# Mixture-of-experts loop reordered: up product of item k+1 between up and down of item k, in two banks; second half of the gather behind the first up product

## What is computed

```python
def layer_norm(x, g, b):
    mu = jnp.mean(xf, -1, keepdims=True)
    var = jnp.mean(jnp.square(xf - mu), -1, keepdims=True)
    ...
def hier_moe(h, w_coarse, w_fine, w1, w3, w2):
    ...
    gates = jnp.einsum('tk,tke->te', w_top, jax.nn.one_hot(expert, MOE_EXPERTS, dtype=jnp.float32)).astype(x.dtype)
    hid = jax.nn.silu(jnp.einsum('td,edf->tef', x, w1)) * jnp.einsum('td,edf->tef', x, w3)
    y = jnp.einsum('tef,efd->td', hid * gates[:, :, None], w2)
    return y.reshape(b, l, d)
# per layer: x <- LN(alpha*x + gate1 * MIX(mod1(x))); x <- LN(alpha*x + gate2 * HMOE(mod2(x)))
# 32 experts, 2 chosen for each token, D_MODEL 1024, hidden width 256
```

## Time and profile before

| | us |
|---|---|
| median of 3 runs | 1191.67 |
| lowest and highest | 1188.70, 1193.04 |
| profiled execution | 1184.91 |
| its span in the trace | 1182.9 |

### The profile page before, as it was taken

How to read it: one execution, slowest core, us unless ns; L and a number is a source line. 1 busy time by engine, 2 the same in 40 slices (tenths; PEclk the granted TensorE clock), 3 DMA queues, 4 the chain that set the end, 5 groups by cost and what they waited for, 6 DMA issues and landing times.

```text
span 1182.9 us, 18088 instructions
## 1 busy us (share of the span) xinstructions
PE 1092.0 (92%) x6858; PEld 766.2 (65%) x6869; DVE 617.9 (52%) x1216; ACT 456.2 (39%) x818; POOL 67.2 (6%) x113
## 2 busy tenths in 40 slices
PE   4999999999989899999979999999998989999993
PEld 0777778787775556665558776878776555555551
DVE  0654757788654532222278385678866353222224
ACT  0634454454343223333354345635524322333332
POOL 0401000200100000000020001010000000000000
PEclk8899999999999999999989999999999999999997
DMA  9997774554899999999977876555376899999991
GB/s 352 308 334 268 269 285 148 179 197 177 322 407 408 411 408 409 409 409 409 378 212 247 306 282 249 178 181 191 139 272 265 315 410 394 410 409 409 408 376 37
DMA packets 107980, 360.08 MB, mean 304 GB/s; under 512 B 9220, under 2 KB 12768, under 8 KB 99696
## 3 DMA queue, kind: packets, MB, share of 16 engines
q1 hardware_dynamic: 97392, 301.48, 67.1%
q0 software_dynamic: 10496, 57.39, 14.0%
HBM read 356.13 MB, written 3.74 MB: 304 GB/s over the span
## 4 chain that ended last, share of the span: by engine, by line
PE 64%; DVE 14%; ACT 7%; issue 5%; DMA 5%; DVEq 3%; ACTq 1%; SPq 0%; POOL 0%; PEld 0%; POOLq 0%
PE bank L923 60%; PE bank L926 4%; DVE wl L1885 3%; ACT wh L1560 3%; DMA first<-in_w_ada 2%; ACT hidT L1832 2%; DMA raw<-in_w_in 1%; DMA adaw<-in_w_ada 1%; DVE merged L1885 1%; DVEq L2232 1%; DVE tmp L1885 1%; DVE seg L2356 1%; DVE tmp L2216 1%; DMA decay<-decay_rows 1%; DVE xbc L2151 0%
## 5 line engine op out<-in xcount | busy, mean ns | idle before, releaser
L1885 DVE TENSOR_TENSOR wl<-raw,wh 128x2048 fp32r<-128x2048 f32 (+1 forms) x76 | 169.1, 2236 | 61.5 <-ACT wh L1560 60.3
L1560 ACT ACTIVATE wh<-raw 128x2048 fp32r<-128x2048 f32 (+1 forms) x76 | 142.6, 1877 | 68.6 <-PE bank L923 48.4
L923 PE MATMUL bank<-wh,hTh 128*128 128x512 f32 x448 | 127.1, 406 | 0.5 <-ACT merged L1582 0.5
L923 PE MATMUL bank<-raw,xg 128*64 128x256 f32 x1088 | 125.1, 381 | 0.0
L923 PE MATMUL bank<-wh,hTl 128*128 128x512 f32 x448 | 121.4, 393 | 0.0
L923 PE MATMUL bank<-wl,hTh 128*128 128x512 f32 x448 | 120.0, 390 | 0.0
L923 PEld LDWEIGHTS bank<-raw,xg 128*64 128x64 f32 x1088 | 93.3, 138 | 39.8 <-issue 17.5
L923 PE MATMUL bank<-wide,xg 128*64 128x256 f32 x1024 | 116.9, 379 | 0.0
L2522 DVE TENSOR_SCALAR selT<-bank 128x256 fp32r<-128x256 f32 x66 | 28.0, 425 | 164.5 <-ACTq L1807 164.5
L923 PEld LDWEIGHTS bank<-wide,xg 128*64 128x64 f32 x1024 | 88.3, 137 | 35.9 <-issue 15.7
L923 PEld LDWEIGHTS bank<-wh,hTl 128*128 128x128 f32 x448 | 85.4, 191 | 18.8
(11 more groups left out here) (328 smaller groups left out, 1473.9 us busy)
## 6 DMA issues: line engine op xcount, KB each, us to landing
raw<-in_moe_w SPq DMA_DIRECT2D x136, 512.0 KB, 11.4
wide<-in_moe_w SPq DMA_DIRECT2D x128, 512.0 KB, 11.6
raw<-in_w_in SPq DMA_DIRECT2D x52, 1024.0 KB, 6.7
wide<-in_moe_w SPq DMA_DIRECT2D x34, 1024.0 KB, 12.9
adaw<-in_w_ada POOLq DMA_DIRECT2D x32, 1024.0 KB, 7.0
raw<-in_moe_w SPq DMA_DIRECT2D x32, 1024.0 KB, 12.6
raw<-in_w_branch SPq DMA_DIRECT2D x12, 1024.0 KB, 5.4
raw<-in_w_ada SPq DMA_DIRECT2D x8, 1024.0 KB, 9.9
```

The source lines that it names most:

```text
L923: return behind(nc.tensor.matmul(*args, **kw))
L1560: A_(wh[c][:, 0:n], raw[:, r, 0:n], ACT.Copy).then_inc(part_high[c], 1)
L1885: return V.tensor_tensor(o, a, b, op)
```

## The change

- **PE** runs up(k+1) between up(k) and turn_hidden(k), into one of two banks by turns; all of its 33 items stand ahead of the branch. At the start only the first half of the gather stands ahead of up(0). The second follows it, and item 0 is finished before up(1).
- **ACT** has all four copies of the second half, take_seats(1) and weigh(0) ahead of sil(0), and in the loop hidT(k-1), sil(k), take_seats(k+2), ygh(k-1), weigh(k+1). `next_piece(0)` stands between the items 31 and 32, as before, but hidT(31) and ygh(31) are now part of item 32's turn.
- **DVE** has low_part(k-1) (ygl) in item k, and the counts of tiles in seven lumps over items 5 to 11.
- **SP** counts a handed back piece by three counters: the first half of up, up, and down. The order of the pieces becomes 0, 1, 3, 4, 2, 6, 7, 5, 9, 10, 8, 12, 13, 11, 15, 16, 14 and so on, with 98 last. The slots are placed anew, so slot 11 is first filled by piece 11, behind 12 and 13.
- **POOL** waits in layer 1 for hT_ready ahead of its parameter loads. **Output** finishes stream 0, then the two halves of stream 1, and DVE's normalisation of stream 1 goes half by half.

```diff
-HIGH_SLOT, LOW_SLOT, RAW_SLOT = (4, 6, 2), (5, 7, 3), 8
+HIGH_SLOT, LOW_SLOT, RAW_SLOT = (6, 8, 2), (7, 9, 10), (3, 4, 5, 11)
...
-DOWN_BANK, UP_BANK, SELECT_BANK = 5, 6, 7
-GATHER_BANKS = (UP_BANK, 0, 1, DOWN_BANK)
+DOWN_BANK, SELECT_BANK = 5, 7
+UP_BANKS = (6, ADA_BANK)
+GATHER_BANKS = (UP_BANKS[1], 0, 1, DOWN_BANK)
...
-        slot = [raw4[:, :], raw5[:, :]] + [wide[i][:, :] for i in (4, 5, 0, 1, 2, 3)] + [raw[:, i, :] for i in range(SLOTS)]
+        slot = ([raw4[:, :], raw5[:, :], wide[4][:, :]] + [raw[:, i, :] for i in range(SLOTS - 1)]
+                + [wide[i][:, :] for i in (0, 1, 2, 3, 5)] + [raw[:, SLOTS - 1, :]])
...
-                return pieces_used, 3 * self.items + j + 1
+
+                k, h = j // 3, j % 3
+                return (pieces_used, up_done, down_done)[h], self.items + k + 1
+
+            def piece(self, at):
+
+                if at < 2 or at == 3 * self.n - 1:
+                    return at
+                return at + 1 if at % 3 != 1 else at - 2
...
-                for j in range(first, end):
+                for at in range(first, end):
+                    j = run.piece(at)
...
-                        sp.wait_ge(*mains[l].finished(RAW_SLOT + i))
+                        sp.wait_ge(*mains[l].finished(RAW_SLOT[i]))
...
+                    pool.wait_ge(hT_ready, 5 * l + 5)
...
+                output((0,), 0, (0, 1), False)
+                output((0,), 1, (0, 1), True)
+                output((1, 2, 3), 0, (0, 1), False)
+                output((1, 2, 3), 1, (0,), False)
+                output((1, 2, 3), 1, (1,), True)
...
+                def gather_second():
...
-                    t = bank[UP_BANK]
+                    t = bank[UP_BANKS[k % 2]]
...
-                    hand_back()
...
-                def items(run, first, end):
-
-                    for k in range(first, end):
-                        up(run, k)
-                        if run.first == 0 and k == 0 and l < L - 1:
-                            pe.wait_ge(room_filled, 2 * QUARTERS * (l + 1))
-                            turn_mod(l, 0, "adaT_next")
+                def items(run):
+
+                    up(run, 0)
+                    if run.first == 0:
+                        gather_second()
+                    if run.first == 0 and l < L - 1:
+                        pe.wait_ge(room_filled, 2 * QUARTERS * (l + 1))
+                        turn_mod(l, 0, "adaT_next")
+                    turn_selected(run, 1)
+                    for k in range(run.n):
+                        if k and k + 1 < run.n:
+                            up(run, k + 1)
+                        turn_hidden(run, k)
                         if k:
                             scatter(run, k - 1)
-                        else:
-                            turn_selected(run, 1)
-                        turn_hidden(run, k)
-                        if k and k + 1 < run.n:
-                            turn_selected(run, k + 1)
                         down(run, k)
+                        if k == 0:
+                            up(run, 1)
+                        if k + 2 < run.n:
+                            turn_selected(run, k + 2)
 
                 def one_more():
-                    items(lasts[l], BRANCH_AT, MAIN)
                     scatter(main, MAIN - 1, True)
-                    pe.sem_inc(pieces_used, 3 * MORE)
+                    pe.sem_inc(pieces_used, MORE)
...
-                        gathered(1, 0)
                         act.drain()
                         act.wait_ge(slots_known, l + 1)
                         act.sem_inc(waited, 1)
@@ -1818,23 +1841,40 @@
                         act.wait_ge(need_ready, l + 1)
                     take_seats(run, 0)
                     if run.first == 0:
-                        for p in range(1, QUARTERS):
+                        for p in range(QUARTERS):
                             gathered(1, p)
                     act.drain()
+                    take_seats(run, 1)
                     weigh(run, 0)
 
+                def hidden_turned(run, k):
+
+                    act.wait_ge(hid_turned, run.items + k + 1)
+                    A_(hidT[:, :], bank[UP_BANKS[k % 2]][:, 256:256 + P], ACT.Copy).then_inc(hidT_ready, run.step(k, MAIN - 1))
+
+                def high_rows(run, k):
+
+                    act.wait_ge(down_done, run.items + k + 1)
+                    A_(ygh[:, :], bank[DOWN_BANK][:, :], ACT.Copy).then_inc(y_high, run.step(k, MAIN - 1))
+
                 def items(run, first, end):
 
                     for k in range(first, end):
+                        if k:
+                            hidden_turned(run, k - 1)
                         act.wait_ge(up_done, run.items + k + 1)
-                        A_(sil[:, :], bank[UP_BANK][:, 0:P], ACT.Silu).then_inc(sil_done, run.step(k, MAIN - 1))
-                        act.wait_ge(hid_turned, run.items + k + 1)
-                        A_(hidT[:, :], bank[UP_BANK][:, 256:256 + P], ACT.Copy).then_inc(hidT_ready, run.step(k, MAIN - 1))
+                        A_(sil[:, :], bank[UP_BANKS[k % 2]][:, 0:P], ACT.Silu).then_inc(sil_done, run.step(k, MAIN - 1))
+                        if k + 2 < run.n:
+                            take_seats(run, k + 2)
+                        if k:
+                            high_rows(run, k - 1)
                         if k + 1 < run.n:
-                            take_seats(run, k + 1)
                             weigh(run, k + 1)
-                        act.wait_ge(down_done, run.items + k + 1)
-                        A_(ygh[:, :], bank[DOWN_BANK][:, :], ACT.Copy).then_inc(y_high, run.step(k, MAIN - 1))
+
+                def last_rows(run):
+
+                    hidden_turned(run, run.n - 1)
+                    high_rows(run, run.n - 1)
...
                     items(lasts[l], BRANCH_AT, MAIN - 1)
                     next_piece(0)
                     items(lasts[l], MAIN - 1, MAIN)
+                    last_rows(lasts[l])
                     next_piece(1)
...
+                    else:
+                        for h in range(2):
+                            hs = slice(h * 512, (h + 1) * 512)
+                            t = bank_full(dve, l, f"{out}1{h}")
+                            frees(tt(tmp[:, hs], t[:, :], gains[:, 1, hs], ALU.mult), f"{out}1{h}")
+                            drain()
+                            V.scalar_tensor_tensor(out=x[:, 1, hs], in0=x[:, 1, hs], scalar=ALPHA, in1=tmp[:, hs], op0=ALU.mult, op1=ALU.add)
+                            drain()
+                            sampled(1, h)
...
                     for k in range(first, end):
                         dve.wait_ge(sil_done, run.items + k + 1)
-                        V.scalar_tensor_tensor(out=hid[:, :], in0=bank[UP_BANK][:, P:2 * P], scalar=gg[:, k % 2:k % 2 + 1], in1=sil[:, :],
+                        V.scalar_tensor_tensor(out=hid[:, :], in0=bank[UP_BANKS[k % 2]][:, P:2 * P], scalar=gg[:, k % 2:k % 2 + 1], in1=sil[:, :],
                                                op0=ALU.mult, op1=ALU.mult).then_inc(hid_ready, run.step(k, MAIN - 1))
                         if last_item and k == end - 1:
                             last_item()
                         if run.first == 0 and k == 0 and l < L - 1:
                             modulation(l, 0, "adaT_next")
-                        if k + 1 < run.n:
-                            selected(run, k + 1)
+                        if k:
+                            selected(run, k)
                         if k + 2 < run.n:
                             weigh(run, k + 2)
-                        dve.wait_ge(y_high, run.items + k + 1)
-                        tt(ygl[:, :], bank[DOWN_BANK][:, :], ygh[:, :].bitcast(F32), ALU.subtract).then_inc(y_low, run.step(k, MAIN - 1))
+                        if k:
+                            low_part(run, k - 1)
                         if run.first == 0 and 1 <= k < 5:
                             done = complete(0, (k - 1) // 2, (k - 1) % 2)
                             if k == 4:
                                 done.then_inc(x_full, 1)
-                        if run.first == 0 and 5 <= k < 8:
-                            (tiles, tile_places, tile_gates)[k - 5]()
+                        if run.first == 0 and k == 5:
+                            tile_opening()
+                        if run.first == 0 and k == 6:
+                            tile_ends()
+                        if run.first == 0 and k == 7:
+                            tile_members()
+                        if run.first == 0 and k in (8, 9):
+                            tile_places(k - 8)
+                        if run.first == 0 and k == 10:
+                            tile_gates()
+                        if run.first == 0 and k == 11:
+                            tile_lists()
```

More of the change, by code:

```diff
@@ L1316, in _, with output @@
-                output((0,), (0, 1))
-                output((1,), (0, 1))
-                output((2, 3), (0, 1))
```

(46 more changed lines are left out.)

77 lines of the change are left out of this document (34 added, 43 removed).

## The result

The changed kernel takes 1207.88 us in the median of 4 runs (1202.05 to 1211.86), the kernel before 1190.18 over its 4 runs. The ratio is 1.0153, with a 95% interval of 1.0118 to 1.0189, so it is slower by 18 us; 8 had been forecast. The profiled execution of the changed kernel took 1211.36 us, 3.5 above its median, and that of before 1184.91, some 5 under its own; so the spans are 26.4 us apart where the medians are 17.7 apart. One execution of this study, of e7, took 2172.63 us, far from all the others, and is left out.

The account below looks back on a forecast made before the run. PE's order was taken as the bound, with 5 to 8 us of stream slack. Layer 0's end +8.9 and layer 1 -0.8 gave +8.1 on the median of 1191.67: 1200 us, range 1187 to 1208.

Parts of the forecast that it names:

- What bounds the kernel now: MoE of both layers: PE's order is the bound, with some 5 to 8 us of slack in the weight stream.
- A period of 6.99: PE's item in mid-MoE: waits go, 7.23 less 0.24 gives at most 6.99 us; the stream stays at 7.71.
- The start: MoE starts: ACT's chain delays up(1) to 364.3 and 928.3; layer 0's stream restarts 5.6 us late, including 1.0 for clock.
- The landing of piece 98: Last weight piece of each layer's MoE: lands at 591.0 in layer 0 and 1156.8 in layer 1.
- The end of layer 0: ACT's q0 copy blocks item 31; last scatter 14.6 us behind piece 98's landing, at 605.6, 8.9 later than before.
- Layer 1: End of layer 1's MoE: down(32) starts at 1158.8 against 1159.63, a gain of 0.8 us.
- Small parts: Finer counters, POOL's wait and output order: taken at nothing; POOL's wait 1 to 2 us if not hidden.
- B: Rival, end of layer 0: q0 isn't late for ACT; layer ends at 597 as before, total about 1191; chance 0.12.
- C: Rival, starts: shorter ACT chain, no hole in the stream; total 1181 to 1183; chance 0.14.
- D: Rival: small hole of 2 us, block at layer 0's end as summed; total about 1192 to 1194; chance 0.08.
- E: Rival, both starts: PE's clock low for longer, slow stream restart; 4 us more a layer, 1208 or above; chance 0.10.
- main case: Whole kernel: late stream restart and q0 block as summed; 1195 to 1207 us; chance 0.56.

Follow-up runs that it names:

- e7: Kernel before with tile counts in seven lumps, new output order and normalisation half by half, without the new item order: 1184.2 us, ratio 0.9949.
- e4: Kernel before with only the tile counts on DVE spread over items 5 to 11 in seven lumps: 1183.53 us, ratio 0.9952.
- e6: Changed kernel, gather's second half ahead of up(0), q0 copy behind hidT(32), up(1) ahead of item 0's down, piece 11 ahead of 12 and 13: 1176.49 us, ratio 0.9894.
- e9: Changed kernel with unread products of constants in PE's gaps at the start of each MoE: 1199.29 us, ratio 1.0082.
- e1: Changed kernel with ACT's copy of q0 behind hidT(32) and its remainder wl behind ygl(32): 1201.14 us, ratio 1.0094.
- e8: Changed kernel with only piece 11 loaded ahead of pieces 12 and 13: 1208.69 us, ratio 1.0154.
- e10: Changed kernel with the tile counts in three large parts, as before the change: 1206.55 us, ratio 1.0146.
- e11: e6 with the tile counts in three large parts, as before the change: 1175.29 us, ratio 0.9895.
- e2: Changed kernel with the second half of the gather ahead of up(0) again: 1191.46 us, ratio 1.0006.

## Why the prediction was off

**What bounds the kernel now: right.** PE ended both layers behind the stream. e4 shows it from the other side: PE's stall taken away, the kernel is 6 us faster, most of it in layer 1. It also bears out why the copy of q0 did no harm before, "since PE trailed": with PE less late it waits 4.54 in the old order too.

**A period of 6.99: wrong, without consequence.** The step took the wait of 0.24 off 7.23. The wait went and the period stayed at 7.22, as the products and turns stand further apart instead. PE is busy through the whole window of e6. PE still caught up with the stream, which needs 7.7 for an item's three pieces, as the step said.

**The start: the mechanism right, the clock mis-sized.** The chain was 15.6 from up(0) to up(1), and the changed kernel's profile has 18.5; up(0) at the lower level adds 1.7 and down(0) 1.7, and with these off it is 15.1, which is also what layer 1 of e9 has at full clock. So ACT's chain was summed to half a microsecond. The failed term is "some of it at the lower of its two levels (1.2 GHz); I add 1.0". The lower clock held for the gather's first half, up(0), down(0) and a part of up(1). In the profile that is 1.5 + 1.7 + 1.7 + 1.0, near 6 a layer, and e9 gives some 8 us for both layers in the medians though it leaves the gather's first half as it is. I had asked only what PE does behind its idle time at the end of the chain, not whether its clock would be low from the gather on.

The stream restarted at 379.9 in layer 0, 7.5 behind the 372.4 of the forecast (371.4 and the 1.0), and 6.5 behind it in layer 1. In layer 0 these 7.5 are 1.8 from ahead of the MoE, 4.8 of the clock, and 1.4 by which the first transfer behind the hole landed later than summed, less the half microsecond of the chain. So the clock is the largest part of what was missed, and in the medians, where 10 us lie between forecast and result, e9 says the same.

Some of it is the draw of the execution. The changed kernel's four runs took 1211.36 and 1211.86 us at a mean granted clock of 0.963, and 1204.39 and 1202.05 at 0.969 and 0.971. The profile is one of the two slower ones, with up(0) at the lower clock in both layers, so it shows more loss than the median has. In this execution 1.8 of the shift in layer 0 arose ahead of the MoE, in code that the change doesn't touch; the start of the gather lay between 342.0 and 346.5 in the profiles of this study.

**The landing of piece 98: right in form.** Behind the first landing the 84 pieces took 220.6 and 220.2 (218.6 and 220.4 taken). The landing is late because the start is.

**The end of layer 0: right.** ACT waited for q0, hidT(31) stood behind it, and the last scatter came at T + 16.7 for T + 14.6. The difference is the clock again: down(31) 3.68 for 1.94 and down(32) 2.96, where 0.8 had been taken for all. e1 gave back 7 us in the medians.

**Layer 1: wrong sign.** A gain of 0.8 had been forecast, and down(32) is 6.3 later beyond the shift of layer 0. Most of it is the clock at the start: the restart was taken at 936.4, 4.4 behind that of before, and was 10.9 behind it beyond the shift (963.4 - 932.0 - 20.5). Of the 1.7 for the normalisation the profile has 0.9, as the gather starts at 927.35 against 907.77 + 20.5, which is less than the stretch from the last scatter of layer 0 to there varies between the profiles (308.0 to 315.0).

**Small parts.** SP's order (e8) and the lumps (e10, e11) count nothing in the changed kernel, as taken. What the output order gives is too small for these runs to tell (e7). POOL's wait wasn't tried.

**The rivals.** B, C and D needed q0 in time or no hole, and neither came. The result lies at the edge of E (1208 or above), which had the mechanism, a lower clock for longer, at 0.10; it deserved more, since the main case already had PE idle for microseconds in a stretch with little work ahead of it.

Of the Trainium skill's 358 GB/s for transfers from HBM (DMA: Bandwidth & Descriptors, section Where 436 GB/s comes from) no run shows a sign: on the one core that the kernel uses, e6 streams 408 and 409 GB/s through the middle of both layers.

## What to carry to other kernels

Before a piece of work is moved off the front of a pipeline, ask what it kept running: here the second half of the gather brought PE to its full clock ahead of up(0) and gave ACT time, and moving it behind up(0) opened a gap in PE, in the clock and in the stream at once. A queue entry that was harmless because its engine ran late (the copy of q0) becomes a block when the order ahead of it changes, or when the engine is late no more (e4); list what stands behind each wait for a transfer in the new order. Two edits that remove the same stall don't add, so test each of them in the old order and in the new one: the new item order with the gather and q0 put back, up(1) early and piece 11 first is 1.1% faster than the kernel before, with or without the lumps.

## What was not expected of the hardware

- The granted clock over 344 to 376 was 0.79 on average in the changed kernel, against 0.99 in e6; at 0.5 for the lower level that is 13 of the 32 us. Idle time ahead of up(0) doesn't settle it by itself: with 2.22 us of it up(0) took 5.33 in the changed kernel, and with 2.24 it took 3.67 in layer 0 of e8. In the seven profiled kernels with both halves of the gather ahead of up(0) all fourteen up(0) took 3.67, also where the gather's first products ran slow (3.42 for 16 of them in layer 0 of e2); in the six with the gather divided five of twelve took 5.33 to 5.36. Products that nothing reads made the kernel 8.6 us faster (e9).
- A wait of 0.24 us in each period of PE was not recovered: with no wait left the period was 7.22 instead of 7.23. The cause is open.
